# Seven-product MLP on Trainium2: weight sums made by accumulating transfers, the other sums on VectorE, the squares on ScalarE

## The reference, cut to what matters

```python
D_MODEL = 1024; D_FF = 4 * D_MODEL
...
h = rms_norm_2(x, norm_mlp[l])
x = x + jnp.square(jax.nn.relu(h @ w_up[l])) @ w_down[l]
return rms_norm_2(x, norm_final)
```

## Time and profile before

| | us |
|---|---|
| median of 3 runs | 1298.86 (1298.46 to 1299.02) |
| the profiled execution | 1296.46 |
| its span, first to last instruction | 1294.6 |
| TensorE busy in it | 1217.9 (94%) |
| VectorE busy | 824.0 (64%) |
| ScalarE busy | 597.2 (46%) |
| GpSimd busy | 313.9 (24%) |

### The profile page before, as it was taken

One profiled execution on the slowest core, in us unless ns is written; L12 is line 12 of the kernel. 1 busy time (PEld: TensorE's weight loads), 2 busy tenths in 40 slices (PEclk: granted clock), 3 DMA queues, 4 the chain that ended last, 5 costly groups with the idle time before them and its releaser, 6 DMA issues.

```text
span 1294.6 us, 16087 instructions
## 1 busy us (share of the span) xinstructions
PE 1217.9 (94%) x6066; PEld 1002.4 (77%) x6066; DVE 824.0 (64%) x1107; ACT 597.2 (46%) x1008; POOL 313.9 (24%) x257
## 2 busy tenths in 40 slices
PE   7999999999999989999989999989998998998994
PEld 5878887768888787887878798877976786876873
DVE  5556566855333457672776664445589679689697
ACT  5456685674322346434665453432453343352443
POOL 2024123200000010000241100110157356375284
PEclk9999999999999999999989999999999998999998
DMA  5411334013334443242131455202520700701502
GB/s 174 107 49 50 82 83 113 17 50 98 98 97 139 135 153 97 79 134 65 33 114 50 146 163 158 71 17 66 177 84 1 244 17 16 244 1 50 177 1 81
DMA packets 148234, 120.75 MB, mean 93 GB/s; under 512 B 4865, under 2 KB 123713, under 8 KB 148162
## 3 DMA queue, kind: packets, MB, share of 16 engines
q1 hardware_dynamic: 142672, 106.05, 28.0%
q10 hardware_dynamic: 5490, 13.73, 3.0%
HBM read 115.55 MB, written 4.22 MB: 93 GB/s over the span
## 4 chain that ended last, share of the span: by engine, by line
PE 70%; DVE 19%; ACT 4%; DMA 3%; issue 2%; POOL 0%; ACTq 0%; SPq 0%; DVEq 0%; POOLq 0%
PE lin L868 20%; PE lin L870 19%; PE lin L869 19%; DVE w_lo L2080 10%; DVE u_lo L2080 2%; PE tr L1026 2%; DMA w_raw<-in_w_up 1%; DMA x_m<-in_x 1%; PE sc L1036 1%; PE sc L1038 1%; ACT w_hi L1417 1%; PE tr L1019 1%; ACT w_hi L1969 1%; DMA w_raw<-in_w_xkv 1%; PE lin L1062 1%
## 5 line engine op out<-in xcount | busy, mean ns | idle before, releaser
L868 PE MATMUL lin<-h_hi,w_hi 128*128 128x512 f32 (+1 forms) x848 | 325.1, 383 | 5.0 <-DVE h_lo L2075 4.6
L870 PE MATMUL lin<-h_hi,w_lo 128*128 128x512 f32 (+1 forms) x848 | 317.4, 374 | 0.0
L869 PE MATMUL lin<-h_lo,w_hi 128*128 128x512 f32 (+1 forms) x848 | 317.0, 374 | 0.0
L2080 DVE TENSOR_TENSOR w_lo<-w_raw,w_hi 128x1024 fp32r<-128x1024 f32 x162 | 208.8, 1294 | 165.5 <-ACT w_hi L1417 154.9
L1417 ACT ACTIVATE w_hi<-w_raw 128x1024 fp32r<-128x1024 f32 x162 | 170.5, 1056 | 169.4 <-PE lin L870 48.9
L868 PEld LDWEIGHTS lin<-h_hi,w_hi 128*128 128x128 f32 x848 | 160.0, 189 | 33.9 <-DVE h_lo L2075 5.3
L870 PEld LDWEIGHTS lin<-h_hi,w_lo 128*128 128x128 f32 x848 | 159.8, 188 | 28.7
L869 PEld LDWEIGHTS lin<-h_lo,w_hi 128*128 128x128 f32 x848 | 160.2, 189 | 25.3 <-issue 0.2
L2080 DVE TENSOR_TENSOR w_lo<-wd_b,w_hi 128x1024 fp32r<-128x1024 f32 x32 | 97.9, 3077 | 1.8 <-ACT w_hi L1969 1.8
L2105 DVE TENSOR_REDUCE neg_max<-sc 128x1 f32<-128x128 f32 (+3 forms) x112 | 52.2, 478 | 72.8 <-PE sc L1038 53.1
L705 POOL TENSOR_SCALAR p<-p,rden 128x128 f32<-128x128 f32 (+1 forms) x80 | 54.1, 677 | 167.3 <-DVE rden L2109 118.9
(11 more groups left out here) (347 smaller groups left out, 2441.8 us busy)
## 6 DMA issues: line engine op xcount, KB each, us to landing
w_raw<-in_w_in SPq DMA_DIRECT2D x74, 512.0 KB, 3.9
w_raw<-in_w_up SPq DMA_DIRECT2D x32, 512.0 KB, 4.7
wd_b<-in_w_down SPq DMA_DIRECT2D x24, 512.0 KB, 7.4
w_raw<-in_w_out SPq DMA_DIRECT2D x16, 512.0 KB, 3.6
w_raw<-in_w_xkv SPq DMA_DIRECT2D x16, 512.0 KB, 4.0
w_raw<-in_w_branch SPq DMA_DIRECT2D x8, 512.0 KB, 3.9
w_raw<-in_w_xq SPq DMA_DIRECT2D x8, 512.0 KB, 3.9
w_raw<-in_w_xo SPq DMA_DIRECT2D x8, 512.0 KB, 3.5
```

The lines of the kernel that those rows point to most:

```text
L868: pe.matmul(o, lh, rh, start=start, stop=False)
L869: pe.matmul(o, lh, rl, start=False, stop=False)
L870: return pe.matmul(o, ll, rh, start=False, stop=stop)
L2080: return dve.tensor_tensor(out, x, as_f32(hi), ALU.subtract)
```

## The change

- **Weight sums.** T1 = B11 + B12 gets a buffer of its own (wd_t1) and is made by VectorE in the up stage (`t1_sum`). The three others become transfers within SBUF that add their source to their destination, issued by GpSimd: T3: B12 += B22, T2: B11 += B12, T4: B21 += B11, each in two halves of 512 KB. They can only add, so the signs move to the u sums and to the sums of results.
- **u sums** (`u_sum`) and **sums of partial results** (`add_partial`, `late_partials`) go to VectorE. Two of the latter are put off to groups 3 and 5 of the next chunk (in the last chunk they stand at k = 8 and 11). The first product is now added to x_res by VectorE itself.
- **Squares**: ScalarE squares what its Relu wrote; VectorE's multiplication goes.
- **Order.** S4 takes over the place of A11 in u_hi and u_lo. T2 serves the fourth product, T1 the sixth. The loads of w_down's blocks are queued behind groups 0 to 7 from the second chunk on, one half each, and those of B11 and B12 wait for the transfers T4 and T2 that read them. The first chunk's order has B11's first half earlier. TensorE's fourth product also waits for the first product's sums.

The diff, cut to its core:

```diff
-A11, A12, A22, S1, S2, S3, S4 = range(7)
-B11, B12, B21, B22 = range(4)
+A11, A12, A22, S1, S2, S3 = range(6)
+S4 = A11
+B11, B12, B21, B22, T1 = range(5)
...
-        Product("v", A22, 9, B21), Product("z", S1, 11, B11), Product("q", S4, 12, B22)]
+        Product("v", A22, 9, B21), Product("z", S1, 11, T1), Product("q", S4, 12, B22)]
...
     for it in range(FF_CHUNKS):
         for c in range(8):
             load_half(U["mlp"][8 * it + c], t_source(w_up, it * D + P * c))
-            if c >= 3:
-                for place, part in {3: [(B12, 0)], 4: [(B22, 0), (B12, 1)], 5: [(B22, 1), (B11, 0)],
-                                    6: [(B11, 1), (B21, 0)], 7: [(B21, 1)]}[c]:
-                    load_down(it, place, part)
+            blocks_behind = {3: [(B12, 0), (B11, 0)], 4: [(B22, 0), (B12, 1)], 5: [(B11, 1), (B22, 1)],
+                             6: [(B21, 0)], 7: [(B21, 1)]} if it == 0 else \
+                {0: [(B12, 0)], 1: [(B11, 0)], 2: [(B12, 1)], 3: [(B11, 1)], 4: [(B22, 0)], 5: [(B22, 1)],
+                 6: [(B21, 0)], 7: [(B21, 1)]}
+            for place, part in blocks_behind.get(c, []):
+                load_down(it, place, part)
...
 # GpSimd: weights_sum, u_sum, add_partial and their calls go
+            for it in range(FF_CHUNKS):
                 for part in range(2):
+                    pool.wait_ge(t1_made, 2 * it + part + 1)
+                    pool.wait_ge(wd_loaded[2 * B22 + part], 16 * (it + 1))
+                    pool.dma_start(wd(B12, part), wd(B22, part), accum_op=ALU.add).then_inc(t3_made[part], 16)
+                for part in range(2):
+                    pool.wait_ge(t3_made[part], 16 * (it + 1))
+                    split_done(pool, down_half(it, 0, part))
+                    pool.dma_start(wd(B11, part), wd(B12, part), accum_op=ALU.add).then_inc(t2_made[part], 16)
+                for part in range(2):
+                    pool.wait_ge(t2_made[part], 16 * (it + 1))
+                    split_done(pool, down_half(it, 2, part))
+                    pool.dma_start(wd(B21, part), wd(B11, part), accum_op=ALU.add).then_inc(t4_made[part], 16)
...
 # TensorE, before a product
                     elif n == 2:
-                        pe.wait_ge(dve_evac, DN[G["mlp"][8 * it + 7]])
+                        pe.wait_ge(act_evac, AN[G["mlp"][8 * it + 7]])
                     elif n == 3:
                         pe.wait_ge(m1_copied, 2 * it + 2)
+                        pe.wait_ge(down_read, 16 * it + 2)
...
 # ScalarE, up stage
                     act.activation(u, bank(g), ACT.Relu).then_inc(act_evac, 1)
-                    after_vector(g)
+                    act.wait_ge(act_evac, AN[g])
+                    act.activation(u, u, ACT.Square).then_inc(u_square, 1)
+                    act.wait_ge(u_square, 8 * it + c + 1)
...
 # ScalarE, down stage
                     if k == 1:
+                        if it > 0:
+                            act.wait_ge(partial_added, 6 * it)
...
+                        u_sum_hi(it, 2, S2, (1, 1))
                     elif k == 2:
-                        u_sum_hi(it, 2, S2, (1, 1))
+                        u_sum_hi(it, 1, S1, (1, 0))
                     elif k == 4:
-                        u_sum_hi(it, 1, S1, (1, 0))
-                    elif k == 6:
                         u_sum_hi(it, 3, S4, (0, 1))
...
 # VectorE, new functions
+            def add_partial(it, row, col, name, op, read):
+                for tile in range(2):
+                    x = of_x(row, col)(tile)
+                    dve.wait_ge(down_read, 16 * it + read + tile)
+                    dve.tensor_tensor(x, x, B[name][:, tile, :], op).then_inc(partial_added, 1)
+
+            def t1_sum(it, part):
+                dve.wait_ge(wd_loaded[2 * B11 + part], 16 * (it + 1))
+                dve.wait_ge(wd_loaded[2 * B12 + part], 16 * (it + 1))
+                if it > 0:
+                    split_done(dve, down_half(it - 1, 5, part))
+                dve.tensor_tensor(wd(T1, part), wd(B11, part), wd(B12, part), ALU.add).then_inc(t1_made, 1)
+
+            def u_sum(it, n, out, x, y, op):
+                dve.wait_ge(u_lo_s, UP_SPLITS * it + (5 if n == 0 else 9))
+                if n > 0:
+                    dve.wait_ge(s_made, 4 * it + n)
+                dve.tensor_tensor(u_block(*out), u_block(*x), u_block(*y), op).then_inc(s_made, 1)
...
 # VectorE, up stage
-                    after_scalar(g)
-                    dve.scalar_tensor_tensor(u, bank(g), 0.0, u, ALU.max, ALU.mult).then_inc(dve_evac, 1)
...
+                    if c in ((2, 4) if it == 0 else (1, 2)):
+                        t1_sum(it, (c - 1) // 2 if it == 0 else c - 1)
+                    if it > 0 and c in (3, 5):
+                        late_partials(it - 1, c // 5)
+                    if c == 4:
+                        u_sum(it, 0, (0, 0), (0, 0), (1, 0), ALU.add)
+                    elif c == 5:
                         u_sum_lo(it, 7, S3, (0, 0))
+                    elif c == 7:
+                        u_sum(it, 1, (1, 0), (1, 0), (1, 1), ALU.subtract)
+                        u_sum(it, 2, (1, 1), (0, 0), (1, 1), ALU.subtract)
...
 # VectorE, down stage
-                    if k == 5:
-                        dve.wait_ge(x_added, 4 * it + 1)
-                        add_down(it, 2, of_x(0, 0), of_x(0, 0))
+                    if k == 4:
+                        add_down(it, 0, of_x(0, 0), of_x(0, 0))
+                    elif k == 6:
+                        add_down(it, 2, of_x(0, 0), of_x(0, 0), 1)
                     elif k == 7:
-                        add_down(it, 3, partial("u2"), partial("u2"))
-                        add_down(it, 1, partial("u3"), partial("u2"), 3)
+                        add_down(it, 3, partial("u2"), partial("u2"), op=ALU.subtract)
+                        add_down(it, 1, partial("u3"), partial("u2"), 5)
...
                     behind_down_lo(it, k)
-                    if k == 2:
+                    if k == 1:
+                        u_sum(it, 3, (0, 1), (1, 1), (0, 1), ALU.subtract)
+                    elif k == 2:
                         u_sum_lo(it, 10, S2, (1, 1))
-                    elif k == 4:
+                    elif k == 3:
                         u_sum_lo(it, 11, S1, (1, 0))
-                    elif k == 6:
+                    elif k == 5:
                         u_sum_lo(it, 12, S4, (0, 1))
+                    elif k == 7:
+                        add_partial(it, 1, 0, "u3", ALU.subtract, 7)
```

More of the change, by code:

```diff
@@ L261, in make_plan @@
     for _ in range(FF_CHUNKS):
-        p.t_halves("mlp", "AD", 8)
+        p.t_halves("mlp", "A", 8)
         p.seven_products("down")
@@ L507, in two_blocks_kernel @@
         wd_loaded = [sem(f"wd_loaded{i}") for i in range(8)]
-        t_made = sem("t_made")
+        t1_made = sem("t1_made")
+        t2_made = [sem(f"t2_made{i}") for i in range(2)]
+        t3_made = [sem(f"t3_made{i}") for i in range(2)]
+        t4_made = [sem(f"t4_made{i}") for i in range(2)]
+        u_square = sem("u_square")
         s_made = sem("s_made")
@@ L597, in wd @@
             i = 2 * place + part
+            if place == T1:
+                return B["wd_t1"][:, part, :]
             return B["wd_a"][:, i, :] if i < 2 else B["wd_b"][:, i - 2, :]
@@ L662, in load_down @@
                 else:
-                    last = {B11: 5, B12: 1, B21: 4, B22: 6}[place]
+                    last = {B11: 3, B12: 1, B21: 4, B22: 6}[place]
                     split_done(sp, down_half(it - 1, last, part))
-                    sp.wait_ge(t_made, 8 * (it - 1) + 8)
+                    if place == B11:
+                        sp.wait_ge(t4_made[part], 16 * it)
+                    elif place == B12:
+                        sp.wait_ge(t2_made[part], 16 * it)
                 dst = wd(place, part).rearrange("p (k n) -> p k n", k=2)
@@ L819, in add_partial @@
-            def add_partial(it, n, row, col, partial):
-                x = B["x_res"][:, 2 * row:2 * row + 2, T * col:T * col + T]
-                pool.tensor_tensor(x, x, B[partial][:, :, :], ALU.add).then_inc(x_added, 1)
-                pool.wait_ge(x_added, 4 * it + n + 1)
-            for it in range(FF_CHUNKS):
-                for place in (B22, B12):
-                    for part in range(2):
-                        pool.wait_ge(wd_loaded[2 * place + part], 16 * (it + 1))
-                weights_sum(it, 0, B12, B22, B12, ALU.subtract)
-                pool.wait_ge(u_lo_s, UP_SPLITS * it + 4)
-                u_sum(it, 0, (0, 0), (0, 0), (1, 0), ALU.subtract)
-                split_done(pool, down_half(it, 0, 1))
-                weights_sum(it, 1, B11, B12, B11, ALU.add)
-                pool.wait_ge(u_lo_s, UP_SPLITS * it + 9)
-                u_sum(it, 1, (1, 0), (1, 0), (1, 1), ALU.add)
-                u_sum(it, 2, (1, 1), (1, 1), (0, 0), ALU.subtract)
-                pool.wait_ge(m1_copied, 2 * it + 2)
-                add_partial(it, 0, 0, 0, "u2")
```

(22 more changed lines are left out.)

51 lines of the change are left out of this document (27 added, 24 removed).

## The result

The median fell from 1298.66 us (4 runs, 1297.01 to 1299.02) to **1255.66 us** (4 runs, 1253.70 to 1257.37): ratio 0.9671, 95% interval 0.9653 to 0.9688, that is 43.0 us less. The forecast was 1257.5 with a range of 1254 to 1281. The profiled execution took 1253.7 us, the fastest of the four; its span is 1251.7.

The account below looks back on a forecast made before the run. TensorE should set the time, but VectorE, slowed beside GpSimd's sums, holds it in the down stages. 41.2 us of stall less 1.0 left plus 1.1 of tail gives 41.3; 1298.86 - 41.3 = 1257.5 us, range 1254 to 1281.

Parts of the forecast that it names:

- The stall and its size: In the four down stages TensorE loses 41.2 us against its matmul pace; nearly all of it goes.
- left-over stall: Before the fourth product TensorE still waits 0 to 0.5 us per chunk, 1.0 us in all.
- The cause: In down stages GpSimd's sums reading SBUF stretch VectorE's 128x1024 operations from 1.21 to 3.41 us; TensorE waits for VectorE's queue.
- The walk through the queue: VectorE's operations followed in order from a down stage's start (t = 0): 35 us of work fit in 38.1.
- the tightest place: The first product's pair of sums on VectorE, ending at 15.8, before the fourth product's start at 16.3: 0.5 us of margin.
- The transfers: Six adding transfers of 512 KB per chunk land in 7 to 8 us; T4 costs nothing up to 11.7 us.
- The loads: In the first chunk ScalarE waits 2.7 instead of 0.95 us for the sixth up half; costed at nothing.
- The tail: At the kernel's end VectorE's last pair of sums no longer waits for a GpSimd sum: 1.1 us less.
- Late transfers: Rival: T4 lands after 12 to 21 us, holding ScalarE, then VectorE; 1275 to 1295 us; chance 0.16.
- Transfers as the bound: Rival: adding transfers occupy the transfer engines beyond 10.5 us each; at 12 us, 1335 us; chance 0.10.
- VectorE stays slow: Rival: reading wd_b or GpSimd's issuing slows VectorE in down stages, 23 us slower, 1322 us; chance 0.03.
- Order of loads: Rival: up halves late behind waits, or first chunk short of blocks: 2 to 4 us per chunk, 1260 to 1273; chance 0.07.

Follow-up runs that it names:

- dve_extra: The kernel after with S1's low part made twice on VectorE, ahead of the first product's pair of sums, in each down stage: 1260.76 us.
- w_pool: The kernel after with the three in-place weight sums made by GpSimd instead of by adding transfers: 1283.47 us.
- u_pool: The kernel after with its four u sums per chunk on GpSimd's queue instead of VectorE's: 1273.78 us.
- w_dve: The kernel after with the three in-place weight sums made by VectorE, no adding transfers: 1255.79 us.
- late2: The kernel after with two 512 KB stores to DRAM, each waited for, ahead of T4 on GpSimd's queue in each chunk: 1264.96 us.
- sq_dve: The kernel after with the 32 squares put back on VectorE: 1256.62 us.
- late3: The kernel after with three 512 KB stores to DRAM, each waited for, ahead of T4 on GpSimd's queue in each chunk: 1281.88 us.
- late1: The kernel after with one 512 KB store to DRAM, waited for, ahead of T4 on GpSimd's queue in each chunk: 1257.20 us.

## Why the prediction was right

**The stall and its size.** Right. 41.2 us were to go and 1.0 to stay; 41.03 went (323.87 to 282.84), and what is left is the pure pace of 1248 matmuls. The left-over stall of 1.0 us did not come: each operation takes its 1.14 us of pitch, the pair ends at t = 15.94 (predicted 15.8) and the product starts at 16.32. It was close: of the 0.5 that I called margin 0.25 us is the handover to TensorE (dve_extra), which the walk did not count, 0.14 went with the pair's later end, and 0.13 us was free. That the uncounted handover cost nothing was luck.

**The cause.** Right, and shown by w_pool and u_pool: with GpSimd's sums beside it the same VectorE queue has 3.4 us operations again, without them none, and TensorE's stretch grows by 26.9 and 17.5 us. The opposite, the old order with the sums taken off GpSimd, was not run, so what the new order of the queues gave by itself is open.

**The walk through the queue.** Right to 0.15 us at the places read: w_lo 4 ends at t = 7.9 (7.8), the pair at 15.9 (15.8). The step "VectorE has room" held with more room than was claimed (32.3 us busy in a down stage, not 35), in w_dve with T4's sums on top, and the tightest place was the right one, in dve_extra.

**The transfers.** Right in effect, high in the value: 4.5 to 5.6 us to landing in the median instead of 7 to 8, inside the bounds from the earlier trace rows. Single ones took 4.5 us, in a quiet stretch, to 7.3 us, beside loads in an up stage. The free room was put at landings of up to 11.7 us (t = 19.5). That step looked only at the weight half itself and not at the backlog that a late half leaves on VectorE; late2 puts the end of the room near t = 17.5, so at landings just under 10 us, still twice what is needed. As the transfers were early, the time did not show the error.

By the estimate from the Trainium skill's "DMA: Bandwidth & Descriptors", section "Anatomy of one DMA", with "Collectives: The Full Stack", section "The bandwidth ceiling", an adding transfer would have been 4.4 us; measured are 4.5 to 5.6, and 4.6 for T4's first half. Whether the second read halves the rate is not isolated: a plain store of the size lands in 2.9 us, but no plain copy within SBUF was run.

**The squares.** Costed at nothing, and nearly nothing is what they do: 0.63 us each on ScalarE, no wait. On VectorE they bring one wait of 1.5 us in the kernel after (sq_dve), too little for its times to show, and 0.2% in the kernel before, where I had expected none.

**The loads.** Right in effect, wrong in the size. ScalarE's rows for the sixth and the seventh up half of the first chunk:

```profile
934.03 1.06 ACT L1407 ACTIVATE w_hi<-w_raw 128x1024 fp32r<-128x1024 f32 x1 [1.66 <-DMA w_raw<-in_w_up]
...
939.41 1.06 ACT L1407 ACTIVATE w_hi<-w_raw 128x1024 fp32r<-128x1024 f32 x1 [2.73 <-DMA w_raw<-in_w_up]
```

It waits 1.66 us for the sixth, where 2.7 was forecast and 0.95 was measured before. The block ahead of that half delayed it little: it lands 11.97 us behind SyncE's first load of w_down instead of 11.72, so 0.25 us later and not the 1.77 us of the sum. TensorE has no wait from either half.

**The tail.** 1.12 us, as forecast (1.1).

**The sum.** 41.0 + 1.1 = 42.1 of the span's 42.9; the rest, 0.75 us, is that the first down stage starts earlier (958.01 for 958.76), which is scatter: the control, the same kernel, starts it at 961.85. The 1.8 us between forecast and median are 1.0 for the left-over stall, and otherwise less than this scatter.

**The rivals.** Late transfers: the mechanism exists and has the price forecast, one us per us and chunk (late3), but its point lies near t = 17.5, and T4's first half is there at 13 (issued at t = 8.5; where late1 to late3 show it, it lands 4.65 us later). Transfers as the bound: the share is 0.91 in the first up stage (922.00 to 958.00), 0.64 to 0.67 in the others and 0.39 at most in a down stage, and an adding transfer lands about as soon (4.5 to 5.6 us) as a load of w_down (5.2). With the first up stage that full TensorE still never waited. VectorE stays slow: it did not, for wd_b or anything else. Order of loads: no wait of TensorE.

## What to carry to other kernels

If one operation of an engine has two durations in a trace, look at which other engine works during the slow ones, before counting work. Taking work off the second engine and giving it to the slow one can make both finish sooner. When a transfer replaces a sum, follow not only when its data are wanted but how much the consumer's in-order queue must catch up behind them. And a stall of TensorE of 3 us or more can cost more than its length.
